# A two-block kernel: x delivered already turned, its norm applied at the exits, and the opening's order and queues changed

## The reference

```
h    = rms_norm(x, g_mix)            # x * rsqrt(mean(x*x) + eps) * g_mix
proj = h @ w_in                      # q, c_kv, k_rope, q_gla, k_gla, v_gla, a_gla, r_gla, q_mem, gates
kv_m = rms_norm(mem, g_mem) @ w_mem_kv
gates = sigmoid(gate_logits + b_gate)
o_gla = rms_norm(og, g_gla_out) * silu(r_gla)
```

## Time and profile before

| | |
|---|---|
| median of 3 runs | 927.0 us (926.98 to 927.25) |
| the profiled execution | 928.21 us, span 926.6 us |
| busy DVE | 720.2 us (78%) |
| busy ACT | 534.9 us (58%) |
| busy POOL | 162.7 us (18%) |
| read from HBM | 174.38 MB, 189 GB/s over the span |
| packets under 512 B | 8560 of 100534 |

### The profile page before, as it was taken

One profiled execution on the slowest core, in us unless ns is written; L12 is line 12 of the kernel. 1 busy time (PEld: TensorE's weight loads), 2 busy tenths in 40 slices (PEclk: granted clock), 3 DMA queues, 4 the chain that ended last, 5 costly groups with the idle time before them and its releaser, 6 DMA issues.

```text
span 926.6 us, 13743 instructions
## 1 busy us (share of the span) xinstructions
PE 905.8 (98%) x4668; PEld 731.7 (79%) x4668; DVE 720.2 (78%) x1030; ACT 534.9 (58%) x831; POOL 162.7 (18%) x247
## 2 busy tenths in 40 slices
PE   8999999999999999999999999999999999999996
PEld 7888888777878778888888887666678688888885
DVE  4779476878778778887679788865668879999976
ACT  6775754476766565555333345655674676666633
POOL 8000000216600000110112001650000023444400
PEclk9999999999999999999999999999999999999999
DMA  8856844876653447887598755322245465555572
GB/s 317 204 150 203 275 137 127 282 268 198 182 180 105 142 142 251 270 268 251 174 351 306 249 159 185 122 73 77 92 138 179 150 193 178 171 174 177 173 251 78
DMA packets 100534, 176.16 MB, mean 190 GB/s; under 512 B 8560, under 2 KB 36592, under 8 KB 100352
## 3 DMA queue, kind: packets, MB, share of 16 engines
q1 hardware_dynamic: 93120, 149.87, 50.8%
q0 software_dynamic: 7184, 25.50, 8.3%
q10 hardware_dynamic: 176, 0.08, 0.0%
HBM read 174.38 MB, written 1.05 MB: 189 GB/s over the span
## 4 chain that ended last, share of the span: by engine, by line
PE 57%; DVE 5%; ACT 2%; issue 1%; DMA 1%; DVEq 0%
PE acc L775 49%; PE turned L1257 2%; PE scores L1246 1%; PE turned L867 1%; DVE wlo L1944 1%; PE turned L1359 1%; PE turned L1146 1%; PE turned L1169 1%; PE turned L811 1%; DMA raw<-in_w_out 1%; ACT prob L1796 0%; ACT whi L1399 0%; DVE soft L2649 0%; DVE turn L2031 0%; PE turned L1261 0%
## 5 line engine op out<-in xcount | busy, mean ns | idle before, releaser
L1944 DVE TENSOR_TENSOR wlo<-raw,whi 128x1024 fp32r<-128x1024 f32 (+3 forms) x269 | 346.1, 1306 | 83.2 <-ACT whi L1399 72.6
L1399 ACT CAST whi<-raw 128x1024 fp32r<-128x1024 f32 (+3 forms) x269 | 273.3, 1032 | 161.2 <-PE acc L775 114.5
L775 PE MATMUL acc<-whi,lta_hi 128*128 128x512 f32 (+2 forms) x576 | 163.4, 399 | 0.2 <-DVEq L2521 0.2
L775 PE MATMUL acc<-whi,lta_lo 128*128 128x512 f32 (+2 forms) x576 | 155.8, 385 | 0.0
L775 PE MATMUL acc<-wlo,lta_hi 128*128 128x512 f32 (+2 forms) x576 | 155.4, 385 | 0.0
L775 PEld LDWEIGHTS acc<-whi,lta_hi 128*128 128x128 f32 x576 | 101.2, 188 | 30.6 <-issue 10.5
L775 PEld LDWEIGHTS acc<-whi,lta_lo 128*128 128x128 f32 x576 | 106.9, 188 | 22.3
L775 PEld LDWEIGHTS acc<-wlo,lta_hi 128*128 128x128 f32 x576 | 106.9, 188 | 21.9
L657 POOL DMA_DIRECT2D wm<-in_w_mod x48 | 34.5, 721 | 427.6 <-DVEq L2075 244.6
L775 PE MATMUL acc<-whi,ltb_hi 128*128 128x512 f32 (+1 forms) x268 | 73.2, 391 | 1.1 <-ACT ltb_hi L1857 0.8
L775 PE MATMUL acc<-wlo,ltb_hi 128*128 128x512 f32 (+1 forms) x268 | 71.2, 384 | 1.6 <-DVE wlo L1944 1.6
(11 more groups left out here) (371 smaller groups left out, 1304.5 us busy)
## 6 DMA issues: line engine op xcount, KB each, us to landing
raw<-in_w_in SPq DMA_DIRECT2D x88, 512.0 KB, 4.4
wm<-in_w_mod POOLq DMA_DIRECT2D x48, 512.0 KB, 6.1
raw<-in_w_up SPq DMA_DIRECT2D x88, 256.0 KB, 3.1
raw<-in_w_up SPq DMA_DIRECT2D x32, 512.0 KB, 4.6
raw<-in_w_down SPq DMA_DIRECT2D x32, 512.0 KB, 5.5
raw<-in_w_down SPq DMA_DIRECT2D x44, 256.0 KB, 3.3
raw<-in_w_o SPq DMA_DIRECT2D x8, 512.0 KB, 4.6
raw<-in_w_out SPq DMA_DIRECT2D x8, 512.0 KB, 4.0
```

The lines of the kernel that those rows point to most:

```text
L775: ins = pe.matmul(acc[s][:, t, 0:n], lhs[part][:, kt0 + kk, tok], w[:, u % RING, kk, 0:n], start=(opens and k == 0 and kk == 0 and j == 0) ...
L1399: act.copy(whi[:, s, :, 0:n], raw[:, s, :, 0:n]).then_inc(hi_ready, 1)
L1944: dve.tensor_tensor(wlo[:, s, :, 0:n], raw[:, s, :, 0:n], whi[:, s, :, 0:n].bitcast(F32), ALU.subtract)\
```

## The change

- x comes from the host a second time, turned (`x_t`), in four pieces (`xT`), loaded by SyncE behind MK2's four units. ScalarE and VectorE multiply each piece by `g_mix` and split it, straight from the arena, without the norm's factor. TensorE's transposes of x, VectorE's product with the factor and the wait for it are gone.
- The factor of x is applied wherever a panel of `h` is read: `normed_rows` in place of `evac` (two activations with a scale instead of one) for AQ, GQ, CK, GK, V0, V1 and Q0 to Q2; in the sigmoid and the product of R0 and R1; and in `gate_in_psum` (two scalar_tensor_tensor instead of one sum).
- The memory's rows are loaded with MK2's second and third unit, x's rows with GQ's last two. The squares move accordingly: the memory's between MK2's last casts, x's after MK2's exit. x's root and inverse come before AQ's exit.
- On ScalarE and VectorE the splits of AQ's first two units come ahead of the memory's root and inverse, and so of MK1's exit.
- The memory's turned pieces are issued by ScalarE, with the vectors' columns behind the first. The first weight tile's cast moves from ScalarE to VectorE. ScalarE's first activation is a root.
- AQ's weights are packed on the host (`w_aq`): one load per unit instead of two. The eight loads of gains become one. The convolution's columns, LN's columns and the positions are loaded after AQ in place of after MK2.

```diff
-            for name, view in GAIN.items():
-                pool.dma_start(view, a[name].partition_broadcast(P)).then_inc(ev("gains_landed"), 16)
+            pool.dma_start(gains[:], a["gains"].partition_broadcast(P)).then_inc(ev("gains_landed"), 16)
@@ SyncE
-                    if name == "MK1":
-                        sp.dma_start(memT[:, 2 * k:2 * k + 2, :], a["mem_t"][:, 2 * k:2 * k + 2, :])\
-                          .then_inc(ev(f"memT{k}_landed"), 16)
...
-                    if name == "MK1" and k == units_of(name) - 1:
-                        for t in range(T):
+                    if name == "MK2":
+                        sp.dma_start(xT[:, 2 * k:2 * k + 2, :], a["x_t"][:, 2 * k:2 * k + 2, :])\
+                          .then_inc(ev(f"xT{k}_landed"), 16)
+                        if k in (1, 2):
+                            t = k - 1
                             sp.dma_start(memx[:, t], a["mem"][t * P:(t + 1) * P, :]).then_inc(ev(f"mem{t}_landed"), 16)
-                    if name == "MK2" and k < T:
-                        sp.dma_start(x[:, k], a["x"][k * P:(k + 1) * P, :]).then_inc(ev(f"x{k}_landed"), 16)
+                    if name == "GQ" and k >= units_of(name) - T:
+                        t = k - units_of(name) + T
+                        sp.dma_start(x[:, t], a["x"][t * P:(t + 1) * P, :]).then_inc(ev(f"x{t}_landed"), 16)
@@ TensorE
             panel("MK1", ltb, new="me")
-            for k in range(4):
-                if k == 3:
-                    pe.wait_ge(ev("h_scaled"), T)
-                    turn_tokens("h", work, groups=(0, 1))
-                unit("MK2", k, ltb)
-            turn_tokens("h", work, groups=(2, 3))
+            panel("MK2", ltb)
             panel("AQ", lta, NARROW["AQ"], new="h")
@@ ScalarE
-                    act.wait_ge(ev("first_landed"), 16)
-                    act.copy(whi[:, 0, 0], raw[:, 0, 0]).then_inc(ev("first_hi"), 1)
...
+            for k in range(4):
+                act.dma_start(memT[:, 2 * k:2 * k + 2, :], a["mem_t"][:, 2 * k:2 * k + 2, :])\
+                   .then_inc(ev(f"memT{k}_landed"), 16)
+                if k == 0:
+                    act.dma_start(vcol[:], a["columns"][:, 0:96]).then_inc(ev("columns_landed"), 16)
...
+            for g in range(4):
+                ahead(2 + g)
+                if g >= 2:
+                    row_squares("mem", memx, 0, g - 2)
+                lt_act("h", lta, (g,))
+            ahead(PLAN.unit["AQ"] - 2)
+            ahead(PLAN.unit["AQ"] - 1)
+            sqrt("mem", stat[:, 0, 2:4])
...
             normed_memory("MK1", kvm[:, :, 256:768], COLS)
-            ahead(PLAN.unit["MK2"] + 2)
-            lt_act("h", lta, (0, 1))
-            ahead(PLAN.unit["MK2"] + 3)
-            lt_act("h", lta, (2, 3))
             normed_memory("MK2", kvm[:, :, 768:1280], COLS)
-            evac("AQ", aq[:], NARROW["AQ"])
+            for t in range(T):
+                ahead(last_unit("AQ") + t)
+                row_squares("x", x, 1, t)
+            sqrt("x", stat[:, 1, 2:4])
...
+            def normed_rows(name, dst, n=COLS):
+
+                ahead(last_unit(name) + 1)
+                panel_wait(name)
+                if name == "AQ":
+                    act.wait_ge(ev("x_inverse"), 1)
+                s, _ = PLAN.bank(name)
+                for t in range(T):
+                    ins = act.activation(dst[:, t], acc[s][:, t, 0:n], ACT.Copy, scale=stat[:, 1, 2 + t:3 + t])
+                ins.then_inc(panel_out[s], 1)
...
+            normed_rows("AQ", aq, NARROW["AQ"])
@@ VectorE
+            dve.wait_ge(ev("first_landed"), 16)
+            dve.tensor_copy(whi[:, 0, 0], raw[:, 0, 0]).then_inc(ev("first_hi"), 1)
...
+            for g in range(4):
+                ahead(2 + g)
+                lt_dve("h", lta, col("g_mix", 0, 8), groups=(g,))
+            ahead(PLAN.unit["AQ"] - 2)
+            row_var("mem", 0)
+            ahead(PLAN.unit["AQ"] - 1)
+            inverse("mem", stat[:, 0, 2:4])
+            dve.sem_inc(ev("mem_inverse"), 1)
+            ahead(last_unit("AQ"))
+            row_var("x", 1)
+            inverse("x", stat[:, 1, 2:4])
+            dve.sem_inc(ev("x_inverse"), 1)
             ahead(PLAN.unit["GQ"])
             evacuated("AQ")
+            dve.wait_ge(ev("conv_columns_landed"), 32)
...
-                    frees(name, dve.tensor_tensor(v, p[:], rsig, ALU.mult))
+                    for t in range(T):
+                        ins = dve.scalar_tensor_tensor(v[:, t], p[:, t], stat[:, 1, 2 + t:3 + t], rsig[:, t], ALU.mult, ALU.mult)
+                    frees(name, ins)
...
-                dve.tensor_tensor(p[:], p[:], bias[:, n % 2].unsqueeze(1).broadcast_to([P, T, COLS]), ALU.add)\
-                   .then_inc(gate_in, 1)
+                for t in range(T):
+                    ins = dve.scalar_tensor_tensor(p[:, t], p[:, t], stat[:, 1, 2 + t:3 + t], bias[:, n % 2],
+                                                   ALU.mult, ALU.add)
+                ins.then_inc(gate_in, 1)
```

More of the change, by code:

```diff
@@ L86, in panels @@
     out = [(f"MK{c}", KT, 1) for c in (1, 2)]
-    out += [("AQ", KT, 2)]
+    out += [("AQ", KT, 1)]
     out += [(n, KT, 1) for n in ("GQ", "CK", "GK", "MK0", "V0", "V1", "R0", "R1", "Q0", "Q1", "Q2", "G20", "G21")]
@@ L289, in hybrid_kernel @@
         ln_sums = sb("ln_sums", [P, T, 8])
-        gains = sb("gains", [P, 6 * 64 + DV_GLA + HEADS])
+        gains = sb("gains", [P, sum(n for _, n in GAINS)])
         ROWS, at = {}, 0
@@ L489, in loads_of @@
             if kind == "AQ":
[L490 to L491 removed]
+                return [(0, a["w_aq"][:, UNIT * k:UNIT * k + UNIT, :])]
             if kind == "CX":
@@ L1515, in _, with row_squares @@
                 ahead(g - 2)
-            for name, src, s in (("me", memx, 0), ("h", x[:], 1)):
-                for t in range(T):
-                    act.wait_ge(ev(f"mem{t}_landed" if name == "me" else f"x{t}_landed"), 16)
-                    act.activation(prob[:].rearrange("p a b -> p (a b)"), src[:, t, :], ACT.Square,
-                                   accum_out=stat[:, s, t:t + 1]).then_inc(ev(f"{name}_sum"), 1)
-                    act.wait_ge(ev(f"{name}_sum"), t + 1)
-                    ahead(2 + s * (t + 1))
-            for name, s in (("me", 0), ("h", 1)):
-                sqrt(name, stat[:, s, 2:4])
+            def row_squares(name, src, s, t):
+                act.wait_ge(ev(f"{name}{t}_landed"), 16)
+                act.activation(prob[:].rearrange("p a b -> p (a b)"), src[:, t, :], ACT.Square,
+                               accum_out=stat[:, s, t:t + 1]).then_inc(ev(f"{name}_sum"), 1)
+                act.wait_ge(ev(f"{name}_sum"), t + 1)
+            for g in range(4):
[6 more added lines that the diff above has]
+            sqrt("mem", stat[:, 0, 2:4])
             def normed_memory(name, dst, n):
@@ L2173, in _ @@
                     .then_inc(ev(f"{name}_var"), 1)
-            for name, s in (("me", 0), ("h", 1)):
-                inverse(name, stat[:, s, 2:4])
-                if name == "me":
-                    dve.sem_inc(ev("me_inverse"), 1)
-            for t in range(T):
-                dve.tensor_scalar(work[:, t], x[:, t], stat[:, 1, 2 + t:3 + t], None, ALU.mult)\
-                   .then_inc(ev("h_scaled"), 1)
-            ahead(PLAN.unit["MK2"] + 1)
-            dve.wait_ge(ev("conv_columns_landed"), 32)
-            ahead(PLAN.unit["MK2"] + 2)
-            lt_dve("h", lta, col("g_mix", 0, 8), groups=(0, 1))
-            ahead(PLAN.unit["MK2"] + 3)
-            lt_dve("h", lta, col("g_mix", 0, 8), groups=(2, 3))
-            ahead(PLAN.unit["AQ"])
+            for g in range(4):
[10 more added lines that the diff above has]
+            dve.sem_inc(ev("x_inverse"), 1)
             ahead(PLAN.unit["GQ"])
             evacuated("AQ")
+            dve.wait_ge(ev("conv_columns_landed"), 32)
             views = []
```

69 lines of the change are left out of this document (36 added, 33 removed).

## The result

The changed kernel took 932.24 us (median of 5 runs, 931.08 to 932.45) against 927.0 for the kernel before: ratio 1.0052, 95% interval 1.0041 to 1.0064. Run once more beside the experiments it took 930.76 (6 runs, 929.83 to 931.35), ratio 1.0036, interval 1.0023 to 1.0048. So it is slower by 3.3 to 4.8 us, where the forecast was 924.9. The experiments are read against both ratios; each ratio has its own interval, so a difference of two of them is sure to about 1.5 us only.

A forecast was written before the change was run, and what follows sets the result against it. TensorE, busy for 98% of the span, was taken as the bound. The terms −3.15 + 0.55 + 0.2 + 0.3 = −2.1 us led from the median of 927.0 to 924.9, range 923.2 to 928.0.

The forecast's parts named there:

- The transposes, −3.15: TensorE before AQ: removing sixteen transposes of x and their waits saves 0.85 and 2.3 us, together 3.15 us.
- The start, counted as nothing: First matmul could start 0.35 to 0.65 us earlier; counted as nothing because another engine sets the next term.
- The fourth rival: Opening: memory's pieces on ScalarE's queue push back the first weights, 0.6 us on TensorE after slack; 925.2, chance 0.10.
- The memory's exit, +0.55: Before AQ: TensorE waits 0.55 us for MK1's exit to free AQ's bank; bounds 0 and 3.4.
- The walk: Memory's exit: MK2's last unit lands at about 24.4 at 403 GB/s, and MK1's exit ends at 31.4.
- The second rival: Before AQ: gains' load holds MK2's last unit until 25.8 to 27.3, the hole stays; 926.3 to 927.8, chance 0.22.
- x's rows, +0.2: From AQ's exit to z: x's second tile lands at about 39.7, costing 0.2 us; bounds 0 and 4.5.
- The third rival: x's rows: second tile lands at 44.2, engines stand still, +4.5 us, 929.4, slower than before; chance 0.12.
- The root at the exits, +0.3: Exits and gates split in two: 0.3 us in all, mainly G20's and G01's sums on VectorE; bounds 0 and 1.8.
- The forecast's signs: Hole before AQ near 0.5, x's second square ending near 41, VectorE's small work at 42 to 43, recurrence wait near 0.8.

The follow-up runs named there:

- both kinds of rows early: Changed kernel with the memory's row tiles asked behind MK1's last unit and x's behind AQ's last two units: 926.10 us, ratio 0.9981.
- The two kernels with the opening of before, untouched: Kernel before with only the exits' new form: both engines' halves 928.74 us, ratio 1.0018; VectorE's half alone 928.42 us, ratio 1.0009.
- the kernel with the pieces back: Changed kernel with the memory's turned pieces asked by SyncE again, each ahead of its unit of MK1: 930.11 us, ratio 1.0022.
- the four kernels with these rows early: Changed kernel, memory's rows behind MK1's last unit: alone 928.81 us; with x's rows behind AQ's last units 926.10; adding earlier memory chain 928.40, or SyncE's pieces 925.99.
- the memory's rows early: Changed kernel with the memory's two row tiles asked behind MK1's last unit, not among MK2's units: 928.81 us, ratio 1.0016.
- x's rows early: Changed kernel with x's row tiles asked behind AQ's last two units instead of GQ's last two: 929.93 us, ratio 1.0019.

## Why the prediction was wrong

**The transposes, −3.15: right.** With both kinds of rows early AQ begins 2.46 earlier than before, after a wait of 0.47 that the forecast had at 0.55. From the second unit's start to AQ's it takes 19.78 us where the kernel before took 22.40: without the wait, 3.09 less.

**The start, counted as nothing: a cost in the changed kernel.** The forecast read the earlier trace rows as the normal start, with the unit's last pair at 11.13 and the second unit at 11.60. The two kernels with the opening of before, untouched, begin that unit at 10.51 and 10.84; in the profiled execution of before the pairs ran at 0.85 from start to start until 10.50, where others have 0.46. So its slack of 0.7 ahead of the second unit was that execution's own; in the other two TensorE waits 0.28 and 0.69 for that unit's cast. In all nine profiles with the pieces on ScalarE's queue the second unit begins at 11.27 to 12.21, in the two changed kernels with them on SyncE's at 10.25 and 10.41. The fourth rival had the mechanism, with 0.6 as its size; the kernel with the pieces back was 1.3 to 2.8 faster, 0.6 to 0.8 of it at z, and with the rows early nothing came of it. The Trainium skill, DMA: Bandwidth & Descriptors, "Issuing engines are not separate DMA queues", says that transfers started by different engines interleave on the same 16 engines. By that rule the fourth rival is right about the sharing, and the traces agree: 8:10 moved 401 GB/s with the pieces on ScalarE's queue and 387 with them on SyncE's, and the weights' second unit began at 11.29 and at 10.41.

**The memory's exit, +0.55: the failed step is the landing of MK2's last unit.** The walk moved the last 5.25 MiB ahead of it at 403 GB/s, to land at 24.4; the cast waited for it until 26.17, and the hole before AQ was 2.45. The change had taken a megabyte of rows, which needs no slot of the ring, from behind MK1's last unit and put it among MK2's. Both places lie ahead of MK2's last unit, so a walk by bytes sees no difference. The runs do: in the four kernels with these rows early that unit landed at 23.7 to 24.3, close to the walk's 24.4, and in the seven other profiles of the change at 25.6 to 28.7. The rate fell with them among MK2's units, 290 GB/s in 13:18 against 398, since SyncE asks for a unit only when the split of the one four before it is done and the queue ran low. That is not the whole: with the pieces on SyncE's queue 13:18 ran at 381 and the unit still took 9.9 us from its request on, against 8.2 with the rows early too (with the pieces on ScalarE's: 9.8 against 7.0). What makes this difference no run separates. From the landing on, the walk was right: 7.0 us from landing to the exit's end in the forecast, 6.8 in the trace. The second rival named the landing (25.8 to 27.3) but blamed the gains, whose load is the same in every one of these kernels, and its 926.3 to 927.8 fell short.

**x's rows, +0.2: the failed step is again a landing.** The forecast had the second tile at 39.7; it was asked for at 36.39, not at 34.7, since the late exit delays the splits of AQ's units, and took 7.6 us instead of about 5: 44.0. (By the forecast's own terms, 34.7 and 5.2 of transfer, it would have been 39.9 and the latency.) The third rival had 44.2. Its price of 4.5 us was too high: z lost 1.92, since VectorE's wait for z, 2.05 before and 0.21 now, shrank first. Its chance, 0.12, was too low: the row of 9.1 us in the earlier trace rows was the nearest measured price for exactly this load, and the forecast preferred bytes over the best rate.

**The root at the exits, +0.3: mis-sized.** Measured by itself 0.8 to 2.5 us by the ratio, and 0.6 to 0.7 by the traces, in the recurrence and in two places behind it, twice the forecast's.

**Two terms were one chain.** The late exit delayed AQ's splits, these SyncE's requests, and these x's rows. The terms were summed as if the second began where the first had left nothing behind. The kernel with both rows early is the one whose hole the forecast described, and it ran at 926.10, 1.2 us above 924.9 and within the range (by its ratio, 925.2); the changed kernel lay 4.2 us outside it, and 2.8 when run again. That the former came so close is partly luck: against the other two profiles with the opening of before, which reach z at 53.54 and 54.59, its z at 52.35 is 1.2 and 2.2 ahead and not 2.49, and the exits cost twice their 0.3.

**Where the loss lies.** The changed kernel's span is 3.2 us longer than that of before: 1.9 at z, 0.6 from z to 338, and 0.75 at the wait near 725 (1.22 for 0.47). In its second profile it is 2.7: 2.1, 0.5 and 0.1.

**The forecast's signs.** The recurrence's wait came at 0.79, as it said, and 20:30 sped up from 231 to 272 GB/s. The hole was 2.45 and not near 0.5, the second square of x ended at 45.2 and not near 41, VectorE's small work began at 47.19 and not at 42 to 43, and a wait of 0.23 at 274 appeared that the trace of before does not have.

**Not foreseen:** the half clock, which may follow the hole. In the kernel before, the turn's transposes split the idle time ahead of AQ into pieces of 0.70 and 0.37 us; with them gone it is one hole.

## What to carry to other kernels

When a change moves a load, walk the queue by when each request is sent, not by bytes over the best rate: find which split or cast releases the request, and use the measured landing of that very load as a bound. In this kernel a load that needs no slot of the ring was better placed where the ring had run out of slots, and a long exit on a casting engine better behind the casts that release requests, as long as its bank was free in time. Compare the opening with more than one profiled execution before calling a microsecond in it slack.

## What the runs showed of the hardware

- The clock after a hole. After TensorE had idled 2.44, 2.45 and 2.76 us (x's rows early, the changed kernel, the pieces on SyncE's queue) behind 19 us of work at the full clock, the granted clock fell to 0.50 to 0.70 of 2.4 GHz in the stretches behind; after 2.37 us in the changed kernel's second profile, and after 1.64, 1.25, 0.78 and 0.47, it stayed at 1.00. The same kernel shows either.
- The fall shows after the hole: one, two or three of AQ's groups (of four matmuls) ran at nearly the full pace in these three executions, then three took 0.91 from start to start, and soon they took 0.50 again.
- The first unit's pace at the start is a draw too. Its pairs of matmuls came 0.85 apart until about 10.5 in three profiles (before, the memory's rows early, x's rows early) and 0.46 apart from 8.5 to 9.4 on in the other eleven, with first matmuls at 7.0 to 7.8 in the former and 6.3 to 7.5 in the latter.
- One load's landing varies by microseconds between executions with the same opening: MK2's last unit was cast at 26.09, 26.17, 26.45, 26.55, 27.26 and 28.72 in kernels that differ only behind it. The runs of one kernel of the change spread by 1.1 to 4.6 us, which is of that size.
